# A six-buffer ring for the later modulation weights, and branch products from two split operands, in a two-layer diffusion trunk

## The reference

```
mod   = silu(c) @ w_mod[l] + b_mod[l]           # and the same for c_ctx; 6144 columns, in six parts
h     = rms_norm(x) * (1 + scale) + shift
parts = h @ w_in[l]                             # columns for the mixers A, B, C and for the gates
o_a   = grouped-query attention;  o_b = neighbourhood attention
o_c   = bidirectional gated DeltaNet, in chunks of 64 tokens, from a start state, both directions
br    = [o_a @ w_branch[l,0], o_b @ w_branch[l,1], o_c @ w_branch[l,2]]     # 512 -> 1024 each
x     = x + gate_m * ((sum over n of sigmoid(gate[n]) * br[n]) @ w_out[l])
x     = x + gate_f * (relu(h2 @ w_ffn1[l])**2 @ w_ffn2[l])
```

## Time and profile before

| | |
|---|---|
| median of three runs | 3652.02 us |
| the profiled execution | 3653.98 us |
| its span | 3652.2 us |
| TensorE matmuls busy | 3310.7 us, 91% |
| DVE, ScalarE, GpSimd busy | 37%, 28%, 29% |
| mean granted TensorE clock | 0.951 |
| HBM traffic | 63 GB/s over the span |

### The profile page before, as it was taken

One profiled execution on the slowest core, in us unless ns is written; L12 is line 12 of the kernel. 1 busy time (PEld: TensorE's weight loads), 2 busy tenths in 40 slices (PEclk: granted clock), 3 DMA queues, 4 the chain that ended last, 5 costly groups with the idle time before them and its releaser, 6 DMA issues.

```text
span 3652.2 us, 48891 instructions
## 1 busy us (share of the span) xinstructions
PE 3310.7 (91%) x20731; PEld 2743.6 (75%) x20731; DVE 1348.5 (37%) x1789; ACT 1025.1 (28%) x1622; POOL 1061.6 (29%) x681
## 2 busy tenths in 40 slices
PE   5997787899888999989999979989998989989997
PEld 3877777787666777768888857888977766668886
DVE  3673333323553111242222257644423542232222
ACT  2441111222453111222221134422222531223232
POOL 4232222233020112232223232343332212244443
PEclk7998889999999999989999988999999999989998
DMA  5122223221001222212222221100021023323331
GB/s 204 47 69 93 93 93 116 70 70 55 5 10 61 55 59 64 64 41 65 63 64 64 64 70 41 36 1 1 9 79 35 10 70 87 98 64 98 96 95 58
DMA packets 303656, 231.36 MB, mean 63 GB/s; under 512 B 16784, under 2 KB 275280, under 8 KB 302544
## 3 DMA queue, kind: packets, MB, share of 16 engines
q1 hardware_dynamic: 297360, 204.55, 19.0%
q0 software_dynamic: 3776, 17.91, 1.4%
q10 hardware_dynamic: 2304, 5.77, 0.4%
HBM read 217.19 MB, written 11.98 MB: 63 GB/s over the span
## 4 chain that ended last, share of the span: by engine, by line
PE 83%; DVE 7%; issue 3%; ACT 3%; DMA 2%; POOL 1%; ACTq 0%; DVEq 0%; POOLq 0%
PE ps L395 17%; PE ps L396 17%; PE ps L397 17%; PE ps L743 6%; PE ps L634 4%; PE ps L649 3%; DMA wring<-in_w_mod 2%; PE ps L480 2%; DVE stat L1145 2%; PE ps L501 1%; PE ps L694 1%; PE ps L642 1%; PE ps L681 1%; PE ps L518 1%; PE ps L698 1%
## 5 line engine op out<-in xcount | busy, mean ns | idle before, releaser
L1486 POOL TENSOR_TENSOR wl<-wring,wh 128x1024 fp32r<-128x1024 f32 x264 | 645.3, 2447 | 1397.7 <-ACT wh L894 1397.7
L395 PE MATMUL ps<-hh,wh 128*128 128x512 f32 (+1 forms) x2592 | 949.2, 366 | 90.2 <-DVE hl L1124 77.5
L396 PE MATMUL ps<-hl,wh 128*128 128x512 f32 (+1 forms) x2592 | 916.9, 354 | 0.0
L397 PE MATMUL ps<-hh,wl 128*128 128x512 f32 (+1 forms) x2592 | 916.3, 354 | 0.0
L395 PEld LDWEIGHTS ps<-hh,wh 128*128 128x128 f32 x2592 | 498.4, 192 | 184.8 <-issue 60.6
L396 PEld LDWEIGHTS ps<-hl,wh 128*128 128x128 f32 x2592 | 499.7, 193 | 73.8 <-issue 9.6
L397 PEld LDWEIGHTS ps<-hh,wl 128*128 128x128 f32 x2592 | 498.3, 192 | 67.3
L894 ACT ACTIVATE wh<-wring 128x1024 fp32r<-128x1024 f32 x264 | 278.1, 1054 | 881.4 <-DMA wring<-in_w_in 433.5
L1421 DVE SCALAR_TENSOR_TENSOR R<-ps,modcs,R 128x512 f32<-128x512 f32 x216 | 136.4, 659 | 389.6 <-PE ps L397 388.6
L396 PE MATMUL ps<-fl,wh 128*128 128x512 f32 (+1 forms) x768 | 274.8, 358 | 0.0
L397 PE MATMUL ps<-fh,wl 128*128 128x512 f32 (+1 forms) x768 | 274.5, 357 | 0.0
(11 more groups left out here) (223 smaller groups left out, 4523.1 us busy)
## 6 DMA issues: line engine op xcount, KB each, us to landing
wring<-in_w_ffn SPq DMA_DIRECT2D x128, 512.0 KB, 3.9
wring<-in_w_in SPq DMA_DIRECT2D x116, 512.0 KB, 3.8
wring<-in_w_mod SPq DMA_DIRECT2D x83, 512.0 KB, 4.6
wring<-in_w_branch SPq DMA_DIRECT2D x48, 256.0 KB, 4.3
wring<-in_w_out SPq DMA_DIRECT2D x16, 512.0 KB, 4.3
x_store<-R POOLq DMA_DIRECT2D x2, 3072.0 KB, 9.7
R<-x_store POOLq DMA_DIRECT2D x2, 3072.0 KB, 10.9
R<-in_w_mod SPq DMA_DIRECT2D x7, 512.0 KB, 13.5
```

Of the source, the lines that this page charges most:

```text
L395: mm(ps[:, t0:t1], ahk, rh[:, k, t0:t1], start=(k == 0), stop=False)
L396: mm(ps[:, t0:t1], ahk, rl[:, k, t0:t1], start=False, stop=False)
L397: last = mm(ps[:, t0:t1], alk, rh[:, k, t0:t1], start=False, stop=(k == kn - 1))
L1486: G.tensor_tensor(slot_view(wl, n % NSPL, l, name, i), w, slot_view(wh, n % NSPL, l, name, i).bitcast(F32), ALU.subtract)\
```

## The change

Three things are done. The split weights' memory becomes one tensor of six slots, which `wh` and `wl` share; the 80 late modulation slots leave the ring `wring` and go through these six, loaded by SyncE when the last z product is done, and the split of the qa slots waits for the last modulation product. The branch products become split products as the others are: their weights go through `wh` and `wl`, and the operands `oA`, `oB`, `oC` are split into `ohi` (ScalarE) and `olo` (DVE, in place of the operand). The order of the pairs becomes branch C, then A, then B, each for all eight output blocks. As `ohi` lies in part where `x` comes back to, the reload moves to pair 18.

```diff
+        wboth = sb("wboth", [P, 2 * NSPL, SLOT])
+        wh, wl = (nc.alloc_sbuf_tensor_at(n, [P, NSPL, SLOT], F32R, offset=w_at + 4 * NSPL * SLOT * i) ...)
+        branches = (2, 0, 1)
+        ohi = [... offset=r_at + 4 * o ... for n, o in enumerate((24576, 16896, 21504))]
+        olo = [... offset=r_at + 4 * o ... for n, o in enumerate((3072, 6144, 0))]
+        late = [(0, i) for i in range(16, 48)] + [(1, i) for i in range(48)]
+        late_in = [sig(f"late_in{i}") for i in range(2 * NSPL)]
@@ plan
-                if l == 0:
-                    for i in range(16, 48):
-                        yield mod_slot(0, i)
-                    for i in range(48):
-                        yield mod_slot(1, i)
                 for i in range(24):
-                    dc, n = divmod(i, 3)
+                    n, dc = branches[i // 8], i % 8
...
-                                           .rearrange("(k p) n -> p k n", p=P))], False
+                                           .rearrange("(k p) n -> p k n", p=P))], True
@@ raw_weights
+            if name == "mod" and (l, i) in late:
+                n = late.index((l, i))
+                eng.wait_ge(*late_in[n % (2 * NSPL)].at(n))
+                return late_home(n)
@@ TensorE, for x in range(24)
-                    w = raw_weights(pe, l, "br", x)
-                    ps = take(pe, "br", l, x)
-                    for t0, t1 in ((0, LAT), (LAT, TOK))[:1 if nt == LAT else 2]:
-                        for k in range(4):
-                            last = mm(ps[:, t0:t1], w[:, k, :], (oA, oB, oC)[x % 3][:, k, t0:t1],
-                                      start=(k == 0), stop=(k == 3))
-                    last.then_inc(*filled("br", l, x))
+                    n = branches[x // 8]
+                    project(("br", l, x), weights(pe, l, "br", x), nt, rhs=(ohi[n], olo[n]), kn=4,
+                            ready=(lambda k: dve_done.at("olo", l, n, k)) if x % 8 == 0 else None)
@@ SyncE, over the slots
+                if (l, name, i) == (0, "qa", 0):
+                    sp.wait_ge(*full("z", 0, 3))
+                    for m, (lm, im) in enumerate(late):
+                        if m >= 2 * NSPL:
+                            ... # wait for TensorE's last use of late[m - 6]
+                        sp.dma_start(late_home(m), mod_slot(lm, im)[4][0][2])\
+                            .then_inc(*late_in[m % (2 * NSPL)].mark(m, by=16))
@@ ScalarE, high
+                    if slot == (0, "qa", 0):
+                        act.wait_ge(*full("mod", *later_mods[-1]))
@@ ScalarE, gate stage
+                act.wait_ge(*dve_done.at("o", l, len(att_pairs(l)) - 1))
+                for k in range(4):
+                    branch_high(l, 2, k)          # A(ohi[n][:, k], o[n][:, k], ACT.Copy)
                 for x in range(24):
...
+                    if 1 <= x < 9:
+                        branch_high(l, (x - 1) // 4, (x - 1) % 4)
@@ DVE, gate stage
+                for k in range(4):
+                    branch_low(l, 2, k)           # olo[n][:, k] = o[n][:, k] - ohi[n][:, k]
                 for x in range(24):
-                    dc, n = divmod(x, 3)
+                    n, dc = divmod(x, 8)
...
+                    if 1 <= x < 9:
+                        branch_low(l, (x - 1) // 4, (x - 1) % 4)
@@ GpSimd
-                for i in range(2):
-                    split(l, "gate", i)
+                split(l, "gate", 0)
+                split(l, "br", 0)
...
-                pool.wait_ge(*pe_done.at("O", l, len(work) - 1))
-                pool.dma_start(R[:, XT0:RN], x_store).then_inc(*x_back.mark(l, by=16))
-                for i in range(2, 24):
+                for i in range(1, 24):
                     split(l, "gate", i)
+                    split(l, "br", i)
+                    if i == 18:
+                        pool.wait_ge(*full("br", l, 15))
+                        pool.dma_start(R[:, XT0:RN], x_store).then_inc(*x_back.mark(l, by=16))
```

More of the change, by code:

```diff
@@ L114, in program @@
         wring = sb("wring", [P, NRAW, SLOT])
-        wh, wl = (ctx.enter_context(nc.sbuf_tensor(n, [P, NSPL, SLOT], F32R)) for n in ("wh", "wl"))
+        w_at = nc.sbuf_base if not callable(nc.sbuf_base) else nc.sbuf_base()
+        w_at = (w_at + 31) // 32 * 32
+        wboth = sb("wboth", [P, 2 * NSPL, SLOT])
+        wh, wl = (nc.alloc_sbuf_tensor_at(n, [P, NSPL, SLOT], F32R, offset=w_at + 4 * NSPL * SLOT * i)
+                  for i, n in enumerate(("wh", "wl")))
         cst = sb("cst", [P, C_N])
@@ L129, in program @@
                   for n, o in (("fh", 0), ("fl", 2 * GF * TOK)))
+        branches = (2, 0, 1)
+        ohi = [nc.alloc_sbuf_tensor_at(f"ohi{n}", [P, 4, TOK], F32R, offset=r_at + 4 * o)
+               for n, o in enumerate((24576, 16896, 21504))]
+        olo = [nc.alloc_sbuf_tensor_at(f"olo{n}", [P, 4, TOK], F32R, offset=r_at + 4 * o)
+               for n, o in enumerate((3072, 6144, 0))]
         PS = [ctx.enter_context(nc.psum_tensor(f"ps{i}", [P, 1024], F32)) for i in range(4)]
@@ L356, in mod_home, with late_home @@
             return r(1024 * (i - NRAW) if i < 12 else 16896 + 1024 * (i - 12), 2, 512)
+        def late_home(n):
+            return wboth[:, n % (2 * NSPL), :].rearrange("p (k n) -> p k n", k=2)
         def raw_weights(eng, l, name, i):
+            if name == "mod" and (l, i) in late:
+                n = late.index((l, i))
+                eng.wait_ge(*late_in[n % (2 * NSPL)].at(n))
+                return late_home(n)
             if l == 0 and name == "mod" and NRAW <= i < 16:
@@ L826, in _ @@
             for n, (l, name, i, kn, pieces, _) in enumerate(slots):
+                if (l, name, i) == (0, "qa", 0):
+                    sp.wait_ge(*full("z", 0, 3))
+                    for m, (lm, im) in enumerate(late):
+                        if m >= 2 * NSPL:
+                            lb, ib = late[m - 2 * NSPL]
+                            cb, kk = divmod(ib, 4)
+                            sp.wait_ge(*(pe_done.at("mod", lb, cb, kk) if kk < 3 else full("mod", lb, cb)))
+                        sp.dma_start(late_home(m), mod_slot(lm, im)[4][0][2])\
+                            .then_inc(*late_in[m % (2 * NSPL)].mark(m, by=16))
                 if n >= NRAW:
@@ L1058, in _, with branch_high @@
                 attention_scalar(act, l)
+                def branch_high(l, n, k):
+                    A(ohi[n][:, k, 0:nt], (oA, oB, oC)[n][:, k, 0:nt], ACT.Copy).then_inc(*act_done.mark("ohi", l, n, k))
+                act.wait_ge(*dve_done.at("o", l, len(att_pairs(l)) - 1))
+                for k in range(4):
+                    branch_high(l, 2, k)
                 for x in range(24):
@@ L1398, in _, with branch_low @@
                 attention(l)
+                def branch_low(l, n, k):
+                    dve.wait_ge(*act_done.at("ohi", l, n, k))
+                    V.tensor_tensor(olo[n][:, k, 0:nt], (oA, oB, oC)[n][:, k, 0:nt], ohi[n][:, k, 0:nt].bitcast(F32),
+                                    ALU.subtract).then_inc(*dve_done.mark("olo", l, n, k))
+                for k in range(4):
+                    branch_low(l, 2, k)
                 for x in range(24):
-                    dc, n = divmod(x, 3)
+                    n, dc = divmod(x, 8)
                     dve.wait_ge(*full("br", l, x))
```

## The result

The changed kernel takes 3519.47 us (median of four runs, 3515.43 to 3522.75) against 3651.7 us for the kernel before (now the median of four runs). The ratio is 0.9634, 95% interval 0.9609 to 0.9659: 132 us less, by the interval 125 to 143. 3523 was predicted, in a range of 3505 to 3556. The profiled execution took 3519.28 us, its span is 3517.5.

A forecast was written before the change was run, and what follows sets the result against it. The prediction took TensorE, its work and its idle waits, to bound the kernel. Load wait 67, clock 24, stage's start -4 and branches 42 sum to 129 us off 3653.98: 3525, as a median 3523 us, range 3505 to 3556.

The forecast's parts named there:

- The load wait, 67 us: Layer 0's delta-rule stage: six buffers remove TensorE's 20 waits for modulation loads, 67 us gained, bounds 61.5 to 68.
- the rival of the loads that bind: Bursts of loads at 304 GB/s outlast the step; half of wait and clock stays, 3568 us; chance 0.08.
- The clock, 24 us, range 0 to 28: Layer 0's delta-rule stage: half-clock stretches behind the load waits go, granted clock 0.90 to about 0.95, 24 us gained.
- The rival, that the clock would not come back: Products, not waits, bring the clock down in layer 0's delta-rule stage, so it stays low: 3547 us; chance 0.17.
- The wait at the stage's start, 4 us lost: Delta-rule stage's start: six loads just ahead of `z_store` delay it and TensorE's L612; 4 us lost, between 0 and 8.6.
- first come, first served: At `z_store`: all six late loads, 3.1 MB at 367 GB/s, go first and delay it by 8.6 us.
- The branch products, 42 us: Gate stages: a split branch block takes half a gate block, 4.17 us for 5.16 and 2.74 for 3.44; 42 gained.
- The estimate from three of four passes, 52 us: Branch blocks: three of four fp32 passes bring 5.16 to 3.87 and 3.44 to 2.58 us, saving 52 us; not adopted.
- The splits, 0: Gate stages: splitting branch weights and operands on ScalarE, GpSimd and DVE is covered by TensorE's work; nothing waits, 0 us.
- The end of the stage: Only out 0 is split ahead; out 1's split is covered with 2.4 us to spare, 0 us, bounds 0 to 3 lost.
- The slower rival: Shared ring of split weights bounds the gate stage, each gate and branch block waiting, 274 us: 3797 us; chance 0.03.

The follow-up runs named there:

- the filled waits: Kernel before, with three extra fp32 matmuls ahead of the fourth slot's wait in each of 20 later modulation products: 3628.22 us, ratio 0.993.
- the run with two passes: Changed kernel, but each branch product leaves out the pass of high weights with low operand: 3467.17 us, ratio 0.9488.

## Why the prediction was right

The sum was 67 + 24 - 4 + 42 = 129 us of 3653.98. The profiled executions are 134.7 us apart, and 128.3 of them lie where the sum has its terms. That the total is met so closely is in part luck: the branch term was some 3 us too high, and the 6.3 us elsewhere were not in the sum.

**The load wait, 67 us.** Right. One wait of 1.5 us is left. (The stage is 88.8 us shorter although the first wait grew by 5.0, so wait and clock gave 93.8 us together where 91 were predicted; with the 27.4 us that the filled waits gave the stage, 66 are left for the wait.) It belongs to the last product of the second delta-rule step, at 381 us, which starts 5.9 us after the one before it and not 6.7; I had taken that distance for the same everywhere. The margin was smaller than worked out: "lands after 4.6 us" was the landing time with three in flight; with six the median is 6.1 us, by the changed kernel's profile:

```profile
wboth<-in_w_mod SPq DMA_DIRECT2D x80, 512.0 KB, 6.1
```

More loads under way each take longer to land. That four buffers, enough for one product, leave 16 waits is the same fact, and it suggests that the rival of the loads that bind stood closer than its 0.08.

**The clock, 24 us, range 0 to 28.** Right, and rather low. Lost at half clock went from 44.0 to 12.8 us, which is 31 and above the range; by the time, the run with filled waits gives 25 (20 to 31) for the same term. The comparison with layer 1's stage was the useful row: 0.95 there, 0.96 here now. What is left, 12.8 us, lies in seven stretches: two at the stage's start and one at each of the five step heads where TensorE is idle for 3.3 us until DVE is done. The rival, that the clock would not come back, fell. Its argument from the product at 297.95 us, whose successor ran at full clock in spite of a wait of 3.1 us, is true, and it is not the only one: 14 of the 20 waits are followed by a stretch and six are not. It shows only that a wait of 3 us can pass without one. The Trainium skill, "TensorE: Matmul & The Clock Gate", section on the oscillation of the clock in real kernels, describes just this: a wait for a transfer of 3 to 5 us after a short group of matmuls, and the next group at half rate. The traces agree for 14 of the 20 waits, as with 3.55 us against 2.05.

**The wait at the stage's start, 4 us lost.** Right: 4.11 us became 9.08. The term was the middle of 0 and 8.6 us, so its size is in part luck. `z_store` took 10.1 us to land, and 5.1 when nothing stood beside it. The 8.6 us for first come, first served took all six loads to be ahead of it; by the issue times only three were (261.1 to 262.0 us, `z_store` at 262.1), which is half of that, at most 4.3 us, so the length of the wait can't tell the two orders apart. The landings can: the third load was issued before `z_store` and landed behind it, after 10.8 us (at 272.8 us, `z_store` at 272.1), where it took 5.5 us in the run that holds the loads back. So the two transfers shared the engines. The rule of the Trainium skill, "DMA: Bandwidth & Descriptors", section on queues, rings and completion order, that the engines take turns between the queues, gave 4.3 us, and 5.0 were measured; these landings agree with it.

Together these three terms are the stage's 88.8 us; 87 were predicted.

**The branch products, 42 us.** 23.0 + 16.5 = 39.5 us in the trace, of which 0.7 is a shorter wait at layer 1's first `out` product; the working had 40.6, and the 1.4 us added on top were not there. A pair takes 12.52 us in layer 0 and 8.26 in layer 1; 12.51 and 8.22 were predicted. A branch block is 4.20 us in layer 0, from the first line to the last; exactly half a gate block would be 4.17:

```profile
1058.51 0.39 PE L409 MATMUL ps<-ohi,wh 128*128 128x512 f32 x1
...
1062.71 0.39 PE L409 MATMUL ps<-hh,wh 128*128 128x512 f32 x1
```

The estimate from three of four passes, 52 us, is refuted. In layer 1 a plain product of 512 columns cost 3.44/4 = 0.86 us, and the three split matmuls that replace it cost 3 x 0.228 = 0.68: a fifth less and not a quarter.

**The splits, 0.** Right, except for 0.7 us at layer 1's end (next paragraph). The first operand of layer 0 is ready at 1054.5 us and wanted at 1058.5; DVE's four take 3.57 us:

```profile
1050.90 3.57 DVE L1435 TENSOR_TENSOR olo<-R,ohi 128x768 fp32r<-128x768 f32 x4 [0.91 <-ACT ohi L1085]
```

**The end of the stage, 0, bounds 0 to 3 lost.** The cost is in the bounds, but the cover worked out ("2.4 us to spare") was not there: in layer 1 out 1 waited for its split weights, and still the stretch got shorter.

```profile
3058.25 0.47 PE L409 MATMUL ps<-hh,wh 128*128 128x512 f32 x1 [3.04 <-DVE hl L1455]
...
3064.61 0.50 PE L409 MATMUL ps<-hh,wh 128*128 128x512 f32 x1 [0.67 <-POOL wl L1528]
```

Before, TensorE had waited 3.73 us for the first `hl` and then worked at half clock for more than half of out 0; now it waited 3.04 us and stayed at full clock. DVE's next work, which needs all of out 0, came 4.65 us after its last subtraction before and 1.77 us after it now. The prediction took out 0 to be paced by DVE's eight subtractions, but they take 4.91 us and out 0 took 8.7 (3189.82 to 3198.54); the half clock made it slow. It was that slowness of 2.9 us which would have covered the split. The matmul in question before, and the windows of 14 us at that place, before and after:

```profile
3189.82 0.77 PE L395 MATMUL ps<-hh,wh 128*128 128x512 f32 x1 [3.73 <-DVE hl L1413]
...
3186.00:3200.00 14.00, 10.27 (x33) 8.15 (x33) 7.73 (x11) 6.28 (x10) 4.47 (x3) 0.76 0.56 151
...
3054.00:3068.00 14.00, 10.29 (x45) 7.87 (x44) 7.04 (x11) 7.23 (x11) 5.88 (x3) 1.00 0.13 38
```

This is no chance of one trace: in all eight runs with split branch products the wait is 3.04 or 3.05 us, and in seven of them the clock stays at 1.00 behind it; in the three with plain ones it is 3.27 to 3.85 us, with the clock down each time. The last pair now has one addition of 0.69 us by DVE ahead of the copies, where there were two (1.38 us). The prediction had this gain nowhere.

**The slower rival**, that the shared ring of split weights becomes the bound, is refuted by the 0.7 us above and by the run with two passes.

## What to carry to other kernels

A ring must hold what one consumer takes at once and, beside that, what is in flight while the next comes: with products of four slots 6.7 us apart and loads that take 6.1 us to land in a burst, four buffers left 16 waits, five 7 and six 1. Count the price of a TensorE wait of 3 us with what follows it at half clock (here 67 us of waits and 25 to 31 us behind them), and where a wait can't be taken away, a matmul of no use inside it gives most of that back. When transfers are moved together, look for the one that somebody waits for.

## What the runs showed of the hardware that was not expected

Matmuls whose result nobody reads are nearly free in TensorE's idle time and keep the granted clock at 1.00 over both delta-rule stages (0.96 without them), worth 14 us there and 25 us in the kernel before. One and the same stage differs between two traces by some us with hardly a difference in its waits: 513.9 and 507.5 us with 61.5 and 61.0 us of waits for loads, and 44.0 and 38.1 us lost at half clock. A transfer that somebody waits for is held up as much by three loads on another queue as by six (8.8 and 9.1 us of wait, 4.1 without them), and a load issued before it landed behind it.
